# Three post norms of a transformer kernel, each in two halves of the tokens

## The chip, the cores and the metric

The kernel runs on one core of one Trainium2 chip. Its time is device time in microseconds (us). The engines of the core work side by side and meet only at semaphores: PE is TensorE (matmuls, with the weight loads beside them as PEld), DVE is VectorE, ACT is ScalarE, POOL is GpSimd, SP is SyncE, whose queue issues the DMAs. Before the change three runs took 2310.77, 2310.92 and 2311.61 us; the median is 2310.92 us.

## The reference

The input is 512 tokens of 1024 numbers. Two blocks follow each other. The first has a hybrid mixer, a gated MLP, a convolution block and another gated MLP. The second, which holds the change, is

```python
def second_block(x, ...):
    for i in range(DEPTH):                      # DEPTH = 2
        h = rmsnorm(x, norm_mixer_pre[i])
        if i % N_MIXERS == 0:
            m = diff_attention(h, ...)
        else:
            m = short_conv(h, conv_w_in[j], conv_w[j], conv_w_out[j])
        x = x + rmsnorm(m, norm_mixer_post[i])
        h = rmsnorm(x, norm_mlp_pre[i])
        x = x + rmsnorm(sq_relu_mlp(h, mlp_w_up[i], mlp_w_down[i]), norm_mlp_post[i])
    return x
```

with `rmsnorm(x, g) = x * rsqrt(mean(x*x) + EPS) * g` over the 1024 features of a token, `sq_relu_mlp(x) = square(relu(x @ w_up)) @ w_down` with a hidden width of 4096, and `short_conv(x) = (b * conv3(c * v)) @ w_out`, where b, c and v are the three thirds of `x @ w_in`. A post norm needs the sum of squares over all features of a token, so it can't start for a token before the last feature block of the projection ahead of it is done. Tokens don't depend on each other in a norm.

## The kernel before

Everything lies transposed: features on the 128 partitions in 8 blocks k of 128 (`KB = 8`), the 512 tokens along the free dimension. `h` is the residual stream. A projection is a row of weight tiles; one tile is 128 output features by 1024 inputs. The 384 tiles (`NT`) are streamed from HBM into a ring of four slots (`RING = 4`), so tile n+4 takes the slot of tile n. ACT rounds a tile to its high part `whi` (`split_hi`), DVE subtracts to get the low part `wlo` (`split_lo`). `split_hi(Tile(n))` and `split_lo(Tile(n))` prepare tile n+4; the first waits until PE is done with tile n. An activation is split in the same way into `xh` and `xl` (or `yh` and `yl`). PE takes three matmuls of 512 columns for each block of a tile (hi by hi, hi by lo, lo by hi), 24 for a tile. The result of a tile lies in one of eight PSUM banks.

Each engine runs its instructions in the order in which its function issues them; a wait holds up all that is behind it on that engine. There is no scheduler: the order is the order of the code, and every counter of a semaphore is written out.

The last five stages are mlp0 (64 tiles), sc (the short convolution: 24 tiles in, 8 out), and mlp1 (64 tiles), with a post norm at the end of each. At such an end, before the change:

- PE runs the 8 last tiles (`down`, called by `to_m`), DVE adds each to `m` (`add_to_m`, or `set_m` in sc), ACT squares it, POOL sums the squares into `acc`. After the eighth tile PE adds up over the partitions with a matrix of ones (`row_sum_halves`, L1798 to L1803), ACT makes the root (`inv_rms_halves`), DVE scales `m` and adds it to `h` (`post_norm`, L951 and L955), ACT makes `xh` (`post_stage`, L471 to L476), DVE makes `xl` (`pre_lo`, L922).
- PE starts the next stage with `first_round`: four tiles at once, block by block as blocks of `xh` and `xl` appear, in banks 0 to 3. Six matmuls that compute nothing (`keep_clock(6)`, L1822) stand in front. At its end stands `row_sum` (L1787, L1788), the sum for the next stage's own pre norm.
- PE goes on with `second_round`: tiles 4 to 7 of the stage in banks 4 to 7. The pre norm is applied late, when DVE takes a tile out of PSUM and multiplies it by `rrow`. So DVE can't take out the first tile before the sum of `row_sum` has gone through ACT (L421, L423).
- The next tiles' weights hang on this too. DVE prepares tiles 4 and 5 of the stage ahead of that wait (`AHEAD = 2`). Tile 6 is prepared behind it: in mlp1 after the third tile was taken out and squared (`up`, L1570 to L1578), in sc after the first three tiles were taken out and convolved (`short_conv`, L928 to L1641). In both the instruction is L916.

After the last tile of mlp1 the end of the kernel follows: `last_norm` on DVE, `residual` and `result` on PE (sums with the identity matrix, f32), copies by ACT (L905), additions by POOL, and eight output DMAs of 256 KB on SP (L379).

Of the kernel before, what the change touches and what calls it, by code (L numbers as in the profile page):

```python
# [130 lines left out]
def build(nc, x_t, stream, w_glr, w_gate, vecs, consts, taps, out_t):  # L131
    with ExitStack() as ctx:
# [127 lines left out]
        for n in ("exact_ready sb_sph sb_spl wglr_in wglr_hi wglr_lo q_hi q_lo glt_ready glr_done warm warm_done first_hi first_lo gq_done gate_x gate_act la_ready suf_ready "  # L260
                  "kd_ready kend_ready dec_ready upd_ready state_ready go_ready gsq_ready gsum_ready "
                  "gln_ready grr_ready gt_ready gy_ready silu_r "
                  "sb_sq sb_sum sb_ln sb_rr sb_qn sb_vp sb_z sb_abs sb_exp sb_ln2 sb_sp sb_acc sb_w "
                  "sv_half dv_half sb_o sb_yh sb_yl wo_early wo_added "
                  "taps_in u4_in0 u4_in1 u4_in2 pw_t1 pw_t2 pw_sg pw_u pw_zero u4_act u4_pool cv_pe cv_chain cv_done piv_mm piv_ready cen_ready cen_sq "
                  "ln_s1 ln_acc mean_mm mean_neg mean_sq ln_var cen_again ln_t ln_s "
                  "lam_s lam_e lam_ready "
                  "da_sh da_shs da_rc da_qn da_vh da_s da_max da_exp da_rcp da_r1 da_t da_a da_T da_aT da_o da_sq da_sum "
                  "da_ln da_rr da_ot do_part do_sum sc_u sc_y sc_zero").split():
            s(n)  # L270
        for n in ("ff_silu", "ff_hid", "mlp_hid"):
            s(n)
        for n in ("halves_act", "halves_dve", "sum_half"):
            s(n)
# [21 lines left out]
        BY_HALVES = ("da", "mlp0", "sc", "mlp1")  # L296
# [16 lines left out]
        def _(sp):  # L313
# [57 lines left out]
            for k in range(KB):  # L371

                if k in LAST_PE:
                    sp.wait_ge(h_added_act, LAST_PE.index(k) + 1)
                elif k in LAST_DVE:
                    sp.wait_ge(h_added, 8 * 3 + LAST_DVE.index(k) + 1)
                else:
                    sp.wait_ge(h_added_pool, LAST_POOL.index(k) + 1)
                sp.dma_start(out_t[k * P:(k + 1) * P, :], h[:, k]).then_inc(stored, 16)  # L379
            sp.wait_ge(stored, 16 * KB)  # L380
# [3 lines left out]
        def _(act):  # L384
# [339 lines left out]
            act.wait_ge(s("mean_mm"), 1)  # L724
# [101 lines left out]
            def to_m(t0, which):  # L826

                for k in range(KB):
                    t = Tile(t0 + k)
                    if k == KB - 1:  # L830
                        split_hi(t)
                        last_square_halves(which, t.count)
                    else:
                        act.wait_ge(evac_done, t.count)
                        square_block(which + "_post", k, A["m"][:, k])
                        split_hi(t)
                inv_rms_halves(which, LAST_ROOT if which == "mlp1" else None)
# [11 lines left out]
            def mlp(f, t0):  # L849
# [4 lines left out]
                inv_rms(name, D, preload=False, bank=7)  # L854
# [25 lines left out]
            post_stage("mlp0", "sc", T_SC)  # L880
# [5 lines left out]
            inv_rms("sc", D, preload=False, bank=7)  # L886
# [14 lines left out]
            post_stage("sc", "mlp1", T_MLP1)  # L901
            mlp(1, T_MLP1)
            for n, k in enumerate(LAST_PE):
                act.wait_ge(h_summed, n + 1)
                act.activation(h[:, k], ps[:, LAST_BANK[k]], ACT.Copy).then_inc(h_added_act, 1)  # L905
# [3 lines left out]
        def _(dve):  # L909
# [9 lines left out]
            def pre_lo(name, k):  # L919

                dve.wait_ge(xh_ready, 8 * PRE[name] + k + 1)
# [54 lines left out]
            def last_norm():  # L976

                a = 8 * POST["mlp1"]
                dve.wait_ge(s("halves_act"), half_done("mlp1", "root"))
                dve.scalar_tensor_tensor(A["m"][:, 0, A_HALF], A["m"][:, 0, A_HALF], col("post", a), LAST_ROOT[:, A_HALF],  # L980
                                         ALU.mult, ALU.mult).then_inc(s("halves_dve"), 1)
                dve.wait_ge(rrow_ready, SUM["mlp1_post"] + 1)
                dve.scalar_tensor_tensor(A["m"][:, 0, B_HALF], A["m"][:, 0, B_HALF], col("post", a), LAST_ROOT[:, B_HALF],
                                         ALU.mult, ALU.mult).then_inc(post_t, 1)
                for k in range(1, KB):
                    t = ps[:, 6] if k in LAST_DVE else A["m"][:, k]
                    dve.scalar_tensor_tensor(t, A["m"][:, k], col("post", a + k), LAST_ROOT, ALU.mult,
                                             ALU.mult).then_inc(post_t, 1)
                    if k in LAST_DVE:
                        dve.wait_ge(post_t, a + k + 1)  # L990
                        dve.tensor_tensor(h[:, k], t, h[:, k], ALU.add).then_inc(h_added, 1)


            dve.memset(acc[:], 0.0).then_inc(s("warm"), 1)
# [32 lines left out]
            dve.wait_ge(s("glt_ready"), 1)  # L1027
# [44 lines left out]
            dve.wait_ge(s("sv_half"), 1)  # L1072
# [153 lines left out]
            dve.memset(A["ub"][:, :, 0:PAD], 0.0).then_inc(s("pw_zero"), 1)  # L1226
# [14 lines left out]
            def gated(b):  # L1241
# [3 lines left out]
                dve.wait_ge(s("pw_zero"), 1)  # L1245
# [38 lines left out]
            def pivot():  # L1284
                dve.wait_ge(s("piv_mm"), 1)
# [7 lines left out]
            def sum_values(k):  # L1293

                dve.wait_ge(s("cen_ready"), k + 1)
                if k == 1:
                    dve.wait_ge(s("piv_mm"), 1)
# [60 lines left out]
            dve.wait_ge(s("mean_mm"), 1)  # L1358
            dve.tensor_scalar(A["mu"][:], ps[:, 7], -1.0 / D, None, ALU.mult).then_inc(s("mean_neg"), 1)
            dve.wait_ge(s("mean_neg"), 1)  # L1360
# [13 lines left out]
            for k in range(KB):  # L1374
                dve.wait_ge(s("cen_again"), k + 1)
# [25 lines left out]
            for r in range(2):  # L1401
# [3 lines left out]
                for t in range(TB):  # L1405
                    if r == 1 and t == 0:
                        dve.wait_ge(s("dv_half"), 1)
# [121 lines left out]
            def set_m(t, k, halves=False):  # L1529
                dve.wait_ge(tile_done, t.count)  # L1530
                if halves:
                    dve.tensor_copy(A["m"][:, k, A_HALF], ps[:, t.slot, A_HALF]).then_inc(s("halves_dve"), 1)
                    dve.tensor_copy(A["m"][:, k, B_HALF], ps[:, t.slot, B_HALF]).then_inc(evac_done, 1)
                else:
                    dve.tensor_copy(A["m"][:, k], ps[:, t.slot]).then_inc(evac_done, 1)
                split_lo(t)

            def add_halves(t, k):
                dve.wait_ge(tile_done, t.count)
                for c, done in ((A_HALF, s("halves_dve")), (B_HALF, evac_done)):  # L1540
                    dve.tensor_tensor(A["m"][:, k, c], ps[:, t.slot, c], A["m"][:, k, c], ALU.add).then_inc(done, 1)
                split_lo(t)
# [14 lines left out]
            def mlp(f, t0):  # L1557
# [25 lines left out]
                up(0, 0, AHEAD)  # L1583
                up(0, 1, bank=RING)
# [10 lines left out]
                for k in range(KB - 1):  # L1595
                    add_to_m(Tile(t0 + 56 + k), k)
                add_halves(Tile(t0 + 56 + KB - 1), KB - 1)

            mlp(0, T_MLP0)
            post_norm("mlp0", "sc")  # L1600


            dve.memset(A["uc"][:, :, 0:2], 0.0).then_inc(s("sc_zero"), 1)
# [6 lines left out]
            def short_conv(i, ahead=0):  # L1610
                def bank(c):
                    return c % RING + (RING if i == 0 and RING <= c < 2 * RING else 0)

                for u in range(4):
# [8 lines left out]
                    dve.wait_ge(s("sc_zero"), 1)  # L1623
# [23 lines left out]
            for k in range(KB):  # L1647
                set_m(Tile(T_SCO + k), k, k == KB - 1)
            post_norm("sc", "mlp1")
            mlp(1, T_MLP1)  # L1650
            last_norm()
# [3 lines left out]
        def _(pool):  # L1655
# [57 lines left out]
            for name in ("da_post", "mlp0_post", "sc_post", "mlp1_post"):  # L1713
                sum_squares(name)
            for k in LAST_POOL:
                pool.wait_ge(post_t, 8 * POST["mlp1"] + k + 1)
                pool.tensor_tensor(h[:, k], h[:, k], A["m"][:, k], ALU.add).then_inc(h_added_pool, 1)
# [835 lines left out]
```

## Time and profile before

| | |
|---|---|
| median of three runs | 2310.92 us |
| the profiled execution | 2311.71 us |
| its span, first to last instruction | 2309.9 us |
| around the span | 1.8 us |
| PE busy | 2286.0 us, 99% |
| DVE busy | 1283.1 us, 56% |
| ACT busy | 823.5 us, 36% |
| POOL busy | 96.6 us, 4% |
| granted TensorE clock | 1.000 |

The end of a matmul is modelled in the profile, with the time that it takes to drain, so matmuls overlap in it: a 512-column matmul is shown with 0.39 us, while the next starts 0.23 us after it. How long PE takes for something is therefore read from starts. A 99% busy PE hides gaps in which it waits for a new stage. In the rows, L is the line of the kernel, and `x4` counts instructions that were merged. An f32 matmul with the matrix of ones or the identity is recorded as two (`x2`).

### The profile page before, as it was taken

How to read it: one execution, taken by the hardware profiler on the slowest of the kernel's cores; microseconds unless marked ns; L12 is line 12 of the kernel's file. 1: busy time of each engine (PE TensorE's matmuls, PEld its weight loads, DVE VectorE, ACT ScalarE, POOL GpSimd, SP SyncE). 2: the span in 40 equal slices, each digit the busy share in tenths (PEclk: the TensorE clock that was granted, in tenths of full speed). 3: DMA queues.
4: the chain of work that ended last, by engine and by line, in shares of the span. 5: the costliest groups of instructions: out<-in, count | busy, mean ns of one | idle time of the engine just before them, and what ended most of it. 6: DMA issues, size and time to landing. Idle time of an engine off the chain costs nothing.

```text
span 2309.9 us, 29030 instructions
## 1 busy us (share of the span) xinstructions
PE 2286.0 (99%) x10627; PEld 1836.2 (79%) x10627; DVE 1283.1 (56%) x1680; ACT 823.5 (36%) x1137; POOL 96.6 (4%) x82
## 2 busy tenths in 40 slices
PE   9999999999999999999999999999999999999999
PEld 7876888888865888888887777888887887888887
DVE  5453643444598654444547868554456755654453
ACT  5376532322423532322334555222224223322222
POOL 0000000000000000000004311000001001000002
PEclk9999999999999999999999999999999999999999
DMA  5210332332464233232332112323322332333321
GB/s 199 83 46 28 102 106 93 100 100 91 165 176 110 74 100 98 93 100 91 108 102 72 48 46 74 119 95 96 100 91 68 116 99 73 110 94 98 100 91 55
DMA packets 64792, 220.00 MB, mean 95 GB/s; under 512 B 8576, under 2 KB 8960, under 8 KB 64448
## 3 DMA queue, kind: packets, MB, share of 16 engines
q1 hardware_dynamic: 64704, 218.78, 29.7%
q8 instruction: 61, 1.00, 0.2%
q14 instruction: 27, 0.22, 0.0%
HBM read 208.56 MB, written 2.10 MB: 91 GB/s over the span
## 4 chain that ended last, share of the span: by engine, by line
PE 88%; DVE 5%; ACT 4%; issue 2%; DMA 0%; POOL 0%; SPq 0%; DVEq 0%; ACTq 0%; POOLq 0%
PE ps L1727 82%; PE ps L2169 2%; PE ps L2289 1%; DVE h L955 1%; PE ps L2034 1%; DVE nm L1442 1%; ACT ex L764 1%; ACT whi L392 0%; ACT xh L476 0%; DVE xl L922 0%; DVE wlo L916 0%; PE ps L2049 0%; DVE spl L1109 0%; DVE acc L944 0%; DVE m L951 0%
## 5 line engine op out<-in xcount | busy, mean ns | idle before, releaser
L1727 PE MATMUL ps<-xh,whi 128*128 128x512 f32 x1752 | 691.6, 395 | 2.1 <-DVE wlo L1000 2.1
L1727 PE MATMUL ps<-xh,wlo 128*128 128x512 f32 x1752 | 683.2, 390 | 0.0
L1727 PE MATMUL ps<-xl,whi 128*128 128x512 f32 x1752 | 682.8, 390 | 0.0
L916 DVE TENSOR_TENSOR wlo<-raw,whi 128x1024 fp32r<-128x1024 f32 x380 | 473.5, 1247 | 229.8 <-ACT whi L392 220.5
L392 ACT ACTIVATE whi<-raw 128x1024 fp32r<-128x1024 f32 x380 | 398.7, 1050 | 478.0 <-PE ps L1727 477.0
L1727 PE MATMUL ps<-yh,whi 128*128 128x512 f32 x1116 | 437.6, 392 | 1.5 <-DVE m L1478 1.0
L1727 PE MATMUL ps<-yh,wlo 128*128 128x512 f32 x1116 | 435.0, 390 | 0.0
L1727 PE MATMUL ps<-yl,whi 128*128 128x512 f32 x1116 | 434.8, 390 | 0.0
L1727 PEld LDWEIGHTS ps<-xh,whi 128*128 128x128 f32 x1752 | 329.5, 188 | 78.0 <-issue 6.5
L1727 PEld LDWEIGHTS ps<-xl,whi 128*128 128x128 f32 x1752 | 329.3, 188 | 69.8 <-issue 3.1
L1727 PEld LDWEIGHTS ps<-xh,wlo 128*128 128x128 f32 x1752 | 329.1, 188 | 68.7
L1727 PEld LDWEIGHTS ps<-yh,whi 128*128 128x128 f32 x1116 | 209.7, 188 | 47.6 <-DVE wlo L916 1.8
L1727 PEld LDWEIGHTS ps<-yl,whi 128*128 128x128 f32 x1116 | 209.7, 188 | 43.6 <-issue 0.7
L1727 PEld LDWEIGHTS ps<-yh,wlo 128*128 128x128 f32 x1116 | 209.6, 188 | 43.6
L860 ACT ACTIVATE yh<-mr 128x512 f32 (+1 forms) x64 | 40.5, 633 | 219.2 <-DVE mr L1570 219.2
L1525 DVE TENSOR_TENSOR m<-ps,m 128x512 f32 (+1 forms) x46 | 31.8, 692 | 128.2 <-PE ps L1727 128.2
L1165 DVE TENSOR_TENSOR h<-ps,h 128x512 f32<-128x512 f32 x56 | 38.7, 691 | 113.1 <-PE ps L1727 113.1
L673 ACT ACTIVATE yh<-th 128x512 f32 x44 | 27.8, 632 | 199.0 <-DVE th L1203 199.0
L1570 DVE SCALAR_TENSOR_TENSOR mr<-ps,rrow 128x512 f32<-128x512 f32 x64 | 44.2, 690 | 94.6 <-PE ps L1727 92.6
L928 DVE TENSOR_TENSOR tu<-ps,rrow 128x512 f32<-128x512 f32 x44 | 30.4, 691 | 72.6 <-PE ps L1727 72.6
L669 ACT ACTIVATE ts<-tg 128x512 f32<-128x512 f32 x44 | 27.8, 632 | 110.5 <-DVE tg L928 110.5
L928 DVE TENSOR_TENSOR tg<-ps,rrow 128x512 f32<-128x512 f32 x44 | 30.4, 691 | 59.4 <-PE ps L1727 45.8
(283 smaller groups left out, 1850.5 us busy)
## 6 DMA issues: line engine op xcount, KB each, us to landing
raw<-stream SPq DMA_DIRECT2D x380, 512.0 KB, 3.5
u<-ub SPq DMA_DIRECT2D x118, 67.0 KB, 2.4
tapw<-taps SPq DMA_DIRECT2D x1, 3584.0 KB, 13.1
h<-x_t SPq DMA_DIRECT2D x8, 256.0 KB, 6.5
raw<-stream SPq DMA_DIRECT2D x8, 256.0 KB, 6.5
out_t<-h SPq DMA_DIRECT2D x8, 256.0 KB, 2.0
const<-consts SPq DMA_DIRECT2D x1, 1025.0 KB, 9.1
vec<-vecs SPq DMA_DIRECT2D x1, 180.0 KB, 9.0
```

Source lines behind the costliest of these rows:

```text
L392: act.activation(whi[:, a.slot], raw[:, a.slot], ACT.Copy).then_inc(whi_ready, 1)
L669: act.activation(A["ts"][:, u], A["tg"][:, u], ACT.Silu).then_inc(s("ff_silu"), 1)
L673: act.activation(block_of(yh, i * 2 + u), A["th"][:, u], ACT.Copy).then_inc(yh_ready, 1)
L764: act.activation(A["ex"][:, p, c, 0:kv], ps[:, 2 + 2 * p + c, 0:kv], ACT.Exp, bias=A["nm"][:, p, c:c + 1], accum_out=A["sm"][:, p, c:c + 1])\
L860: act.activation(block_of(yh, i * 4 + j), A["mr"][:, j % 2], ACT.Square).then_inc(yh_ready, 1)
L916: dve.tensor_tensor(wlo[:, a.slot], raw[:, a.slot], whi[:, a.slot].bitcast(F32), ALU.subtract)\
L928: dve.tensor_tensor(dst, ps[:, bank], rrow[:], ALU.mult).then_inc(evac_done, 1)
L1165: dve.tensor_tensor(h[:, k], ps[:, bank], h[:, k], ALU.add).then_inc(evac_done, 1)
L1525: dve.tensor_tensor(block_of(A["m"], k), ps[:, t.slot], block_of(A["m"], k), ALU.add)\
L1570: dve.scalar_tensor_tensor(A["mr"][:, j % 2], ps[:, bank + t.slot], 0.0, rrow[:], ALU.max, ALU.mult)\
L1727: mm = pe.matmul(out, lhs, rhs, start=first and n == 0, stop=last and n == 2, skip_group_check=skip)
L2169: mm = pe.matmul(ps[32 * i:32 * i + 32, 5 + b % 2], tapw[:, b, i, m], A["u4"][:, b % 3, i, SHIFTS * m:SHIFTS * m + T], start=m == 0, stop= ...
```

## The change

It does four things in the ends of mlp0, sc and mlp1, and in the starts of sc and mlp1. The post norm of the attention (da) and the start of mlp0 stay as they are.

1. The last tiles before a post norm (3 in mlp0 and sc, 4 in mlp1; the table `SPLIT`) are computed in two passes of 256 columns: first the A half (tokens 0 to 255) of all of them, then the B half (256 to 511) of all. The sum of squares and the root are made for A while PE works on B.
2. The norm, the addition to `h`, `xh` and `xl` are made for the eight blocks of A, then for those of B (`post_split`). DVE scales and adds block k before it makes `xl` of block k-1.
3. `first_round` of sc and mlp1 is replaced by `split_round`: the A half of three tiles block by block; the fourth tile joins at k = 4, in the code, and catches up four blocks; then the B half of all four tiles. It uses banks 4 to 7, `second_round` banks 0 to 3. The sum for the B half of the post norm stands after block k = 2. The six matmuls of `keep_clock` are not issued there.
4. The sum for the next stage's pre norm is no longer at the end of the first round but in `second_round`, after the first of its four tiles.

At the end of mlp1 the A halves of all eight blocks are normed, added by POOL and stored while PE still works; only the B halves go the old way (DVE, PE, ACT, POOL). There are 16 output DMAs of 128 KB instead of 8 of 256 KB. Some semaphores are merged or renamed, with no instruction added or taken away.

```diff
+        SPLIT = {"mlp0": 3, "sc": 3, "mlp1": 4}
...
+            def post_split(which, t0, following, add):
...
+                for k in range(first, KB):
+                    sum_half(t0, k, which, A_HALF, add)
+                sum_half(t0, first, which, B_HALF, add)
+                norm_a(0)
+                add_a(0)
+                norm_a(1)
+                add_a(1)
+                lo_a(0)
+                split_lo(Tile(t0 + first))
+                sum_half(t0, KB - 2, which, B_HALF, add)
+                norm_a(2)
+                add_a(2)
+                lo_a(1)
+                split_lo(Tile(t0 + KB - 2))
+                sum_half(t0, KB - 1, which, B_HALF, add)
+                for k in range(3, KB):
+                    norm_a(k)
+                    add_a(k)
+                    lo_a(k - 1)
+                    if k == 3:
+                        split_lo(Tile(t0 + KB - 1))
+                lo_a(KB - 1)
+                norm_b(0)
+                add_b(0)
+                for k in range(1, KB):
+                    norm_b(k)
+                    add_b(k)
+                    lo_b(k - 1)
+                    if k > LAG + 1:
+                        sq_sum(following, k - LAG - 1)
...
-            def second_round(t, free, name):
+            def second_round(t, free, name, bank=RING):
 
                 for j in range(RING):
+                    if j == 1 and bank == 0:
+                        pe.wait_ge(evac_done, free)
+                        row_sum(name, bank=3)
                     if j == RING - 1:
                         pe.wait_ge(ln_ready, SUM[name] + 1)
-                    tile(t.plus(j), RING + j, xh, xl, free=free)
+                    tile(t.plus(j), bank + j, xh, xl, free=free)
...
+            def split_round(t0, name, which):
+
+                base, last = X0[name], t0.plus(RING - 1)
+                for k in range(KB):
+                    pe.wait_ge(x_ready, base - KB + k + 1)
+                    for j in range(RING - 1):
+                        if k == 0:
+                            pe.wait_ge(wlo_ready, t0.plus(j).count)
+                        half_passes(t0.plus(j), RING + j, xh, xl, A_HALF, k)
+                    if k == 2:
+                        post_sum(which, B_HALF)
+                    if k == 4:
+                        pe.wait_ge(wlo_ready, last.count)
+                        pe.wait_ge(ln_ready, SUM[which + "_post"] + 1)
+                        for done in range(4):
+                            half_passes(last, 2 * RING - 1, xh, xl, A_HALF, done)
+                    if k >= 4:
+                        half_passes(last, 2 * RING - 1, xh, xl, A_HALF, k)
+                for k in range(KB - 2):
+                    pe.wait_ge(x_ready, base + k + 1)
+                    for j in range(RING):
+                        half_passes(t0.plus(j), RING + j, xh, xl, B_HALF, k)
+                pe.wait_ge(x_ready, base + KB)
+                for j in range(RING):
+                    for k in range(KB - 2, KB):
+                        mm = half_passes(t0.plus(j), RING + j, xh, xl, B_HALF, k)
+                    mm.then_inc(tile_done, 1)
...
             def to_m(t0, which, y0):
-                down(Tile(t0), y0)
-                row_sum_halves(which)
+                first = KB - SPLIT[which]
+                for j in range(first):
+                    tile(Tile(t0 + j), j % RING, yh, yl, y_ready, y0)
+                for c in (A_HALF, B_HALF):
+                    for j in range(first, KB):
+                        t = Tile(t0 + j)
...
+                        for k in range(KB):
+                            mm = half_passes(t, t.slot, yh, yl, c, k)
+                        mm.then_inc(s("tile_half") if c is A_HALF else tile_done, 1)
+                        if c is B_HALF and j == first:
+                            post_sum(which, A_HALF)
+                if which == "mlp1":
+                    post_sum(which, B_HALF)
```

Where the instructions stand shows two places. The first is PE at the join of the first and the second round of sc. Before, the sum for the pre norm (`ps<-sums,exact`) stands between the last matmul of the first round and the first of the second:

```order
L1727 MATMUL ps<-xl,whi 128x512
L1727 MATMUL ps<-xh,wlo 128x512
L1787 MATMUL ps<-sums,exact 128x512 [waits sum_lo]
L1788 MATMUL ps<-sums,exact 128x512
L1727 MATMUL ps<-xh,whi 128x512 [waits evac_done,wlo_ready]
```

Now, in the same stage, the last matmuls ahead of that sum are those of the second round's first tile, and what follows is its second tile:

```order
L1936 MATMUL ps<-xl,whi 128x512
L1936 MATMUL ps<-xh,wlo 128x512
L1996 MATMUL ps<-sums,exact 128x512 [waits sum_lo,evac_done]
L1997 MATMUL ps<-sums,exact 128x512
L1936 MATMUL ps<-xh,whi 128x512 [waits evac_done,wlo_ready]
```

The sum has moved down by the 24 matmuls of one tile; the third tile of the round (tile 6 of the stage) now starts one tile after the sum, where it started two tiles after it. The second place is DVE at the end of mlp0. Before, after the last block's addition in two halves (L1541) and one tile of weights (`wlo`):

```order
L1541 TENSOR_TENSOR m<-ps,m 128x256 [waits tile_done]
L1541 TENSOR_TENSOR m<-ps,m 128x256
L916 TENSOR_TENSOR wlo<-raw,whi 128x1024 [waits whi_ready]
L951 SCALAR_TENSOR_TENSOR m<-m,vec,rrow 128x256 [waits halves_act]
L955 TENSOR_TENSOR h<-h,m 128x256 [waits halves_dve]
L951 SCALAR_TENSOR_TENSOR m<-m,vec,rrow 128x256 [waits rrow_ready]
L955 TENSOR_TENSOR h<-h,m 128x256 [waits post_t]
L951 SCALAR_TENSOR_TENSOR m<-m,vec,rrow 128x512
L922 SCALAR_TENSOR_TENSOR xl<-h,vec,xh 128x512 [waits xh_ready]
```

Now, from the B half of the first of the three split tiles on:

```order
L1062 TENSOR_TENSOR m<-ps,m 128x256 [waits tile_done]
L1074 SCALAR_TENSOR_TENSOR m<-m,vec,rrow 128x256 [waits root_half]
L1079 TENSOR_TENSOR h<-h,m 128x256 [waits post_t]
L1074 SCALAR_TENSOR_TENSOR m<-m,vec,rrow 128x256
L1079 TENSOR_TENSOR h<-h,m 128x256 [waits post_t]
L1083 SCALAR_TENSOR_TENSOR xl<-h,vec,xh 128x256 [waits xh_ready]
L994 TENSOR_TENSOR wlo<-raw,whi 128x1024 [waits whi_ready]
L1062 TENSOR_TENSOR m<-ps,m 128x256 [waits tile_done]
L1074 SCALAR_TENSOR_TENSOR m<-m,vec,rrow 128x256
L1079 TENSOR_TENSOR h<-h,m 128x256 [waits post_t]
L1083 SCALAR_TENSOR_TENSOR xl<-h,vec,xh 128x256 [waits xh_ready]
L994 TENSOR_TENSOR wlo<-raw,whi 128x1024 [waits whi_ready]
```

The weights of the next stage's tiles 1, 2 and 3 (`wlo`, L994) now stand between the halves of the norm, because PE holds their slots until the B half of the down tiles is done.

## Rows read from the trace of the kernel before

**Rows 1.** The page: PE's busy line, and the chain that ended last, by engine.

```profile
PE 2286.0 (99%) x10627; PEld 1836.2 (79%) x10627; DVE 1283.1 (56%) x1680; ACT 823.5 (36%) x1137; POOL 96.6 (4%) x82
...
PE 88%; DVE 5%; ACT 4%; issue 2%; DMA 0%; POOL 0%; SPq 0%; DVEq 0%; ACTq 0%; POOLq 0%
```

**Rows 2.** Timeline of PE, end of mlp0 to sc's second round (start us, duration us).

```profile
1755.83 0.39 PE L1727 MATMUL ps<-yh,whi 128*128 128x512 f32 x1
...
1761.04 0.40 PE L1727 MATMUL ps<-yh,wlo 128*128 128x512 f32 x1
1761.28 0.59 PE L1798 MATMUL ps<-acc,const 128*128 128x256 f32 x2
1761.71 0.60 PE L1799 MATMUL ps<-acc,const 128*128 128x256 f32 x2
...
1766.38 0.28 PE L1840 MATMUL ps<-xh,wlo 128*128 128x256 f32 x1
...
1768.06 0.28 PE L1840 MATMUL ps<-xh,wlo 128*128 128x256 f32 x1
...
1789.14 0.40 PE L1788 MATMUL ps<-sums,exact 128*128 128x512 f32 x1
1789.38 0.39 PE L1727 MATMUL ps<-xh,whi 128*128 128x512 f32 x1
```

**Rows 3.** The same of PE, end of sc to mlp1's second round.

```profile
1941.49 0.40 PE L1727 MATMUL ps<-yh,wlo 128*128 128x512 f32 x1
...
1969.58 0.40 PE L1788 MATMUL ps<-sums,exact 128*128 128x512 f32 x1
1969.81 0.39 PE L1727 MATMUL ps<-xh,whi 128*128 128x512 f32 x1
```

**Rows 4.** Timeline of all engines, post norm of mlp0.

```profile
1762.95 0.70 PE L1801 MATMUL ps<-sq,const 128*128 128x256 f32 x2 [0.65 <-ACT sq L437]
...
1763.69 0.39 ACT L446 ACTIVATE lnb<-ps 128x256 f32<-128x256 f32 x1 [0.48 <-PE ps L1801]
...
1764.56 0.48 DVE L951 SCALAR_TENSOR_TENSOR m<-m,vec,rrow 128x256 f32<-128x256 f32 x1 [0.70 <-ACT rrow L448]
...
1765.08 0.42 DVE L955 TENSOR_TENSOR h<-h,m 128x256 f32<-128x256 f32 x1
1765.42 0.48 DVE L951 SCALAR_TENSOR_TENSOR m<-m,vec,rrow 128x256 f32<-128x256 f32 x1
1765.54 0.51 ACT L471 ACTIVATE xh<-h,vec 128x256 fp32r<-128x256 f32 x1 [0.29 <-DVE h L955]
...
1766.94 0.75 DVE L922 SCALAR_TENSOR_TENSOR xl<-h,vec,xh 128x512 fp32r<-128x512 f32 x1
```

**Rows 5.** Timeline of POOL and DVE: a low part beside POOL, and one without it.

```profile
1757.47 1.30 POOL L1667 TENSOR_TENSOR acc<-acc,sq 128x512 f32<-128x512 f32 x1 [4.15 <-ACT sq L401]
1758.37 1.48 DVE L916 TENSOR_TENSOR wlo<-raw,whi 128x1024 fp32r<-128x1024 f32 x1 [1.65 <-ACT whi L392]
...
1762.63 1.23 DVE L916 TENSOR_TENSOR wlo<-raw,whi 128x1024 fp32r<-128x1024 f32 x1 [0.39 <-ACT whi L392]
```

**Rows 6.** Timeline of DVE: low part of tile 6 in sc and in mlp1.

```profile
1797.96 1.23 DVE L916 TENSOR_TENSOR wlo<-raw,whi 128x1024 fp32r<-128x1024 f32 x1 [0.26 <-ACT whi L392]
...
1977.77 1.23 DVE L916 TENSOR_TENSOR wlo<-raw,whi 128x1024 fp32r<-128x1024 f32 x1 [0.19 <-ACT whi L392]
```

**Rows 7.** The end of the kernel: timelines of PE, DVE, ACT, SP, and the DMAs of L379.

```profile
2296.00 0.40 PE L1727 MATMUL ps<-yh,wlo 128*128 128x512 f32 x1
...
2296.44 0.76 DVE L1541 TENSOR_TENSOR m<-ps,m 128x256 f32<-128x256 f32 x2 [4.76 <-PE ps L1727]
...
2305.51 0.60 ACT L905 ACTIVATE h<-ps 128x512 f32<-128x512 f32 x1 [0.26 <-PE ps L2376]
...
2301.57 5.88 SPq L379 DMA_DIRECT2D out_t<-h  x8
...
DMA to landing us min/median/max: 2.0/2.0/2.5
```

More of the change, by code:

```diff
@@ L826, in to_m @@
             def to_m(t0, which):
-                for k in range(KB):
[L829 to L837, printed above, removed]
+                name, first, root = which + "_post", KB - SPLIT[which], LAST_ROOT if which == "mlp1" else rrow
@@ new lines, in root_b @@
+                def root_b():
+                    act.wait_ge(sum_ready, SUM[name] + 1)
+                    act.activation(lnb[:, B_HALF], ps[:, SUM_BANK, B_HALF], ACT.Ln, scale=1.0 / D, bias=EPS)\
+                       .then_inc(ln_ready, 1)
+                    act.wait_ge(ln_ready, SUM[name] + 1)
+                    act.activation(root[:, B_HALF], lnb[:, B_HALF], ACT.Exp, scale=-0.5).then_inc(rrow_ready, 1)
+                for k in range(first):
+                    act.wait_ge(evac_done, t0 + k + 1)
+                    square_block(name, k, A["m"][:, k])
+                    split_hi(Tile(t0 + k))
@@ new lines, in to_m, with x_a @@
+                for k in range(first, KB):
+                    square_a(k)
+                square_b(first)
+                root_a()
+                if which == "mlp1":
+                    for k in range(first + 1, KB):
+                        square_b(k)
+                    root_b()
+                    return
+                following, tn = {"mlp0": ("sc", T_SC), "sc": ("mlp1", T_MLP1)}[which]
+                pre = 8 * PRE[following]
+                def x_a(k):
+                    act.wait_ge(h_added, NORM[which] - KB + k + 1)
+                    act.activation(xh[:, k, A_HALF], h[:, k, A_HALF], ACT.Copy, scale=col("pre", pre + k)).then_inc(xh_ready, 1)
@@ new lines, in x_b @@
+                def x_b(k):
+                    act.wait_ge(h_added, NORM[which] + k + 1)
+                    act.activation(xh[:, k, B_HALF], h[:, k, B_HALF], ACT.Copy, scale=col("pre", pre + k)).then_inc(xh_ready, 1)
+                split_hi(Tile(t0 + first))
+                x_a(0)
+                x_a(1)
+                split_hi(Tile(t0 + KB - 2))
+                square_b(KB - 2)
+                x_a(2)
+                square_b(KB - 1)
+                split_hi(Tile(t0 + KB - 1))
+                x_a(3)
@@ L1975, in _ @@
             wide(Tile(T_SV + 2), 2, 2, 512)
-            wide(Tile(T_SV + 3), 3, 2, 512, order=(2, 3, 0, 1), half=s("sv_half"))
+            wide(Tile(T_SV + 3), 3, 2, 512, order=(2, 3, 0, 1), half=s("v_half"))
             def gla_sum(hd):
```

310 lines of the change are left out of this document (229 added, 81 removed).

## The prediction, before the changed kernel had run

> **What bounds the kernel now.** I read first the page. PE is busy 99% of the span and carries 88% of the chain that ended last [rows 1]; no other engine is near. The kernel is as long as PE's work plus the places where PE waits, and these hide in the busy share. So I went on to the timeline of PE around the two joins that change and the end, and took everything from starts of instructions.
>
> A 512-column matmul takes PE 5.21 us / 23 = 0.2265 us (first to last of one tile, 1755.83 to 1761.04), a tile 24 of them, 5.44 us [rows 2]. The join of mlp0 and sc: the last down matmul is through at 1761.04 + 0.23 = 1761.27, the second round starts at 1789.38, 28.11 us later [rows 2]. In that time stand the 96 matmuls of the first round, 21.74 us. What is left, 6.37 us, is the price of the join: the sum of squares, root, norm, waits, and the sum for the pre norm. In the second join the last down matmul is through at 1941.72 and the round starts at 1969.81: 28.09 us, 6.35 lost [rows 3]. The end: the last down matmul starts at 2296.00, the span ends at 2309.9, 13.9 us [rows 7]. That is all that the change can win: 12.7 us at the joins, part of 13.9 at the end.
>
> **The price of half matmuls.** 256-column matmuls stand in the old first round: fifteen starts, 14 steps, from 1766.38 to 1768.06 make 0.120 us each [rows 2]. Two halves are 0.240, against 0.2265: 0.0135 more for each pair. At each join (3 x 24) + (4 x 24) = 168 pairs cost 2.3 us; at the end 4 x 24 = 96 cost 1.3 us.
>
> **What PE does and waits for at a join.** I laid a timetable from the start of the first A half (t = 0) with the rows' steps. Three A halves 8.64, the first B half to 11.52, the sum for A (two f32 matmuls of 0.43, the step from 1761.28 to 1761.71 [rows 2]) to 12.38, two B halves to 18.14. The second matmul of the sum starts at 11.95; ACT's log 0.74 later, the norm on DVE 0.87 behind it, the addition 0.52 later, `xh` 0.46 later [rows 4]. So the first norm is at 13.56, the addition at 14.08, and the first A block of `xl` can start at 15.3. DVE's steps in a row are 0.40 for a half norm (0.48 shown, less the 0.08 by which a start precedes the end before it, as 1765.08 + 0.42 to 1765.42 shows [rows 4]) and 0.34 for a half addition; `xl` has the form of the norm (0.75 whole, no half in the trace), so I take 0.40. Bounds for it: 0.34, a half addition, and 0.75, the whole. With the wait of 0.12 between norm and addition that is 1.25 us for a block.
>
> Between them stand three weight tiles of about 1.14 (1.23 shown [rows 5]) and two half additions. Tile 2 of the next stage is ready at 19.65, PE wants it at 18.86: 0.8 us of wait. Block 2 is ready at 21.3, block 3 at 23.9, where PE stands at 23.2 after the sum for B: 0.7. With block 4 the fourth tile gives PE 2.9 us of work at once, and from there to the end of the A part it is ahead of nobody: it leaves A at 32.4. DVE begins B at 28.2, and with the sums of squares of the next norm (0.6 each from k = 5) has the last `xl` at 40.9; PE wants it at 41.0. End of the first round: 43.85, of which 1.8 is waiting. The low part of tile 4 comes 0.5 us after that. The second round starts at 44.35. Before, from the same point: 3 x 5.44 + 28.11 = 44.4. **The two are equal.** All that was hidden has been paid for: 6.37 of lost time became 2.3 for half matmuls, 1.7 for the two sums, 2.3 of waits. On top comes the sum for the pre norm, before inside the 28.11 and now behind tile 4: 0.45. Each join: +0.4 us. POOL's half additions are off this path. Their price isn't in the trace: between half of the 1.30 of a whole one and all of it [rows 5]. The last that PE needs has 3 us to spare.
>
> **What the moved sum makes late.** The sum's second matmul in sc starts at 1789.14; the low part of tile 6, which stands behind the first three tiles' work on DVE, starts at 1797.96 and takes 1.23, so it is there at 1799.19, 10.05 us after the sum [rows 2, 6]. Before, PE ran tiles 4 and 5 in that time, 0.24 + 10.88 us, and tile 6 was 1 us early. Now tile 4 stands ahead of the sum, and only tile 5, 0.23 + 5.44 = 5.67, beside the chain. DVE's and ACT's work between is the same, instruction by instruction. PE waits 10.05 + 0.06 - 5.67 = 4.4 us, and 0.1 that I allow for the slower first matmul after a wait: **4.5 us**. In mlp1 the chain is 1977.77 + 1.23 - 1969.58 = 9.42 us [rows 3, 6]: 9.42 + 0.06 - 5.67 + 0.1 = **3.9 us**. Nothing gives it back, since PE is what bounds. In mlp1 DVE is then 5.4 us later with the eight hidden blocks, each 3.3 us of DVE with its weights, and the first down tile needs the last of them; I count 0.4 for it (bounds 0 and 1.5).
>
> sc +4.9, mlp1 +4.7: +9.6.
>
> **The end.** PE has 1.3 more for halves and 0.86 for the sum for A: +2.15. After the last matmul (X): DVE 0.33, ACT 0.79, the second sum matmul 1.25, log 1.99, first norm 2.85 (0.86 after the log). Eight half norms at 0.40, the last at 5.65, the sixth, k = 5, at 4.85; through PE (f32 halves of 0.43) to ACT, done at 6.6. Before, that copy was done at 2306.11, 10.1 after X, and the span ended 3.8 later: three issues on SP's queue and 2.0 to land [rows 7]. With the same 3.8: 10.4, against 13.9. The A halves are stored before; eight more issues of about 0.35 on SP are through by 2 us after X. So -3.5 + 2.15 = -1.35 (bounds -3 and 0, by 0.64 or 1.3 for POOL's last half addition, and whether half DMAs land as whole ones do).
>
> **Sum.** +9.6 - 1.35 = +8.25; I take +8.3. The span becomes 2318.2 and the profiled execution, 1.8 around the span, 2320.0 us. The profiled execution lay 0.8 above the median of the runs; I give 2319.2 for the median.
>
> **Rivals.**
> A. VectorE is slowed by POOL. The low part took 1.48 with POOL still in the first 0.4 us of it, and 1.23 without [rows 5]: 0.25 lost for 0.4 beside. POOL's half additions (0.65 to 1.30) now fall among DVE's half norms, twice at a join: 0.8 to 1.6 us of DVE in the stretch where PE waits on it, and its half steps may each be some 0.05 longer. Together +2 each join: 2323.2. The Trainium skill (GPSIMD Engine Reference, Specifications) says that GpSimd shares its SBUF interfaces with VectorE, and contends with instructions that have two SBUF inputs. All of the half norms, additions and `xl` have two. The row agrees. For: the row. Against: most of the wait in question is short.
> B. Half matmuls cost just half. Then 0.0135 x 432 pairs = 5.8 us go from PE's work. About half of it comes back as waits, as PE stands before the same DVE blocks in the A part: -2.9, 2316.3. Against it stand 14 equal steps of 0.120. The Trainium skill (TensorE: Matmul & The Clock Gate, Back-to-back issue gap) gives a lone warm matmul N/2.4 + 2.5 ns; that is 2.5 ns for each added one, an estimate of 1.1 us for 432, and nearly this case. The row, 13.5 ns, decides against it.
> C. The other side: the kernel gets faster. The mechanism is the third tile of the second round: if its weights were ready when PE comes (the chain behind the sum short of 5.7 us), the 8.4 us of the two waits fall away, and with them the later DVE work: 8.3 - 8.8 = -0.5, no change. To be faster by more than that DVE must also keep ahead in the A part: another 2.3 of waits at each join, -5.1: 2305.8. It decides at 5.7 us; the chains measure 10.05 and 9.42, so this needs an order of instructions that is not the one built.
> D. The waits come as forecast, but the end wins all it can and the A part waits on nobody: 8.3 - 1.5 - 2.5 = +4.3, 2315.2: at the edge of no change.
>
> **Chances.** Forecast 0.70 (its own range 2317 to 2321.5), A 0.15, B 0.05, D 0.07, C 0.03 with both its forms. A change of 0.2% is 4.6 us; less a measurement of this kernel can't tell. Faster: 0.02. Within 0.2%, up to 2315.5: half of D, part of B and C, 0.06. Slower: 0.92. The range from D to A: 2314.8 to 2323.8.
>
> **What would show it.** In the profile after: PE idle of 4 to 5 us before the first matmul of tile 6 of sc, and just under 4 in mlp1, with the low part (DVE, `wlo`) as what ended it; the old 28.1 us of a join, from the last whole down tile to the second round, equal within 1 us; steps of 0.120 between half matmuls also where one tile runs through its eight blocks; 10.4 us after the start of the last down matmul. I would be wrong if tile 6 finds its weights, if half steps are below 0.115 or above 0.125 (each 0.005 is 2 to 4 us over the kernel), or if PE waits for `xl` in the B part, which has only 0.1 us to spare.

## The result, and the profile after

The changed kernel takes 2323.97 us (median of 6 runs, 2321.14 to 2325.57) against 2311.01 for the kernel before (6 runs, 2310.33 to 2311.61): 13.0 us slower, a ratio of 1.0054 with a 95% interval of 1.0041 to 1.0067. I had forecast 2319.2, +8.3, and slower with 0.92; the time lies 0.2 above the upper end of the range, 2323.8. The direction and the places were right, the size was not: what PE pays behind a long wait was put at 0.1 us, and measured 2.97 and 2.57.

The profiled execution took 2324.94 us, its span 2323.2, 13.3 above the span before. The page's busy line and the chain that ended last, as in [rows 1]:

```profile
PE 2291.8 (99%) x11031; PEld 1859.0 (80%) x11031; DVE 1290.9 (56%) x1738; ACT 829.0 (36%) x1158; POOL 102.2 (4%) x97
...
PE 87%; DVE 7%; ACT 4%; issue 2%; DMA 0%; POOL 0%; SPq 0%; DVEq 0%; ACTq 0%; POOLq 0%
```

PE has 404 matmuls more and is still 99% busy. The new thing is in the chain: VectorE went from 5% to 7%. What PE waits for in the last 620 us says where (idle us in all, how often, the longest):

```profile
PE ps L1936 <- DVE wlo L994: 10.6, 6, 4.2
PE ps L1936 <- DVE xl L1083: 0.9, 2, 0.5
PE ps L2104 <- ACT sq L856: 0.5, 1, 0.5
PE ps L2657 <- DVE m L1160: 0.5, 1, 0.5
```

10.6 us are waits for low parts of weights, in six places. The timeline of PE shows them, first the join of mlp0 and sc, then sc's second round (start us, duration; to be read beside [rows 2]):

```profile
1743.90 0.28 PE L1936 MATMUL ps<-yh,whi 128*128 128x256 f32 x1
...
1763.92 0.39 PE L1936 MATMUL ps<-xh,whi 128*128 128x256 f32 x1 [1.02 <-DVE wlo L994]
...
1768.17 0.38 PE L1936 MATMUL ps<-xh,whi 128*128 128x256 f32 x1 [0.46 <-DVE xl L1083]
...
1788.70 0.50 PE L1936 MATMUL ps<-xh,whi 128*128 128x512 f32 x1 [0.32 <-DVE wlo L994]
...
1794.50 0.39 PE L1997 MATMUL ps<-sums,exact 128*128 128x512 f32 x1
...
1799.99 0.39 PE L1936 MATMUL ps<-xh,wlo 128*128 128x512 f32 x1
1804.59 0.80 PE L1936 MATMUL ps<-xh,whi 128*128 128x512 f32 x1 [4.21 <-DVE wlo L994]
1805.18 0.63 PE L1936 MATMUL ps<-xl,whi 128*128 128x512 f32 x1
...
1810.30 0.63 PE L1936 MATMUL ps<-xl,whi 128*128 128x512 f32 x1
1810.73 0.44 PE L1936 MATMUL ps<-xh,wlo 128*128 128x512 f32 x1
```

From the first A half, 1743.90, to the second round, 1788.70, are 44.80 us; before, from the start of the same three tiles, it was 44.43, to 1789.38 [rows 2]. So the join is equal within 0.4. The sum for the pre norm now stands at 1794.50, behind tile 4, and tile 5 runs until 1799.99 + 0.23. Then PE waits 4.37 us for the low part of tile 6, until 1804.59 (the 4.21 in the row counts from the modelled end of the last matmul). Behind this wait stands what I had not counted: fourteen steps from 1804.59 to 1810.73 take 6.14 us where fourteen of 0.2265 take 3.17. The same in mlp1 (beside [rows 3]):

```profile
1988.98 0.39 PE L1936 MATMUL ps<-xh,wlo 128*128 128x512 f32 x1
1992.96 0.79 PE L1936 MATMUL ps<-xh,whi 128*128 128x512 f32 x1 [3.59 <-DVE wlo L994]
1993.55 0.63 PE L1936 MATMUL ps<-xl,whi 128*128 128x512 f32 x1
...
1998.25 0.54 PE L1936 MATMUL ps<-xh,whi 128*128 128x512 f32 x1
```

A wait of 3.75 us, then twelve steps in 5.29 us where 2.72 would do. The windows of PE say why (stretch, PE busy and matmuls, granted clock, DMA share, GB/s):

```profile
1800.00:1804.00 4.00, 0.38 (x2) 1.00 0.00 0
1804.00:1808.00 4.00, 3.41 (x8) 0.50 0.49 152
1808.00:1812.00 4.00, 4.00 (x13) 0.65 0.71 242
...
1988.00:1992.00 4.00, 1.37 (x7) 0.97 0.00 0
1992.00:1996.00 4.00, 3.04 (x7) 0.50 0.38 131
1996.00:2000.00 4.00, 4.00 (x13) 0.68 0.38 131
```

After the wait the granted clock is 0.50, that is 1.2 instead of 2.4 GHz, and it comes back to 2.4 GHz within the next of these stretches. The matmuls ran at half speed, in steps of 0.427 us.

What holds the low part of tile 6 is the chain on VectorE. Its first and last link in sc:

```profile
1796.23 0.69 DVE L1006 TENSOR_TENSOR cc<-ps,rrow 128x512 f32<-128x512 f32 x1 [5.84 <-ACT rrow L436]
...
1803.31 1.23 DVE L994 TENSOR_TENSOR wlo<-raw,whi 128x1024 fp32r<-128x1024 f32 x1 [0.25 <-ACT whi L405]
```

VectorE stood idle 5.84 us for the root of the pre norm, which needs PE's late sum. The same place before the change:

```profile
1790.87 0.69 DVE L928 TENSOR_TENSOR cc<-ps,rrow 128x512 f32<-128x512 f32 x1 [0.98 <-ACT rrow L423]
```

The low part is ready at 1804.54, 10.04 us after the second matmul of the sum started at 1794.50. Before, this chain was 10.05 [rows 2, 6]: nothing in it changed, it only starts later by one tile of PE's work, 5.4 us.

The end of the kernel, of PE, DVE, ACT and SP (beside [rows 7]):

```profile
2313.23 0.28 PE L1936 MATMUL ps<-yh,wlo 128*128 128x256 f32 x1
...
2315.21 0.38 ACT L868 ACTIVATE lnb<-ps 128x256 f32<-128x256 f32 x1 [0.79 <-PE ps L2104]
...
2316.04 2.83 DVE L1160 SCALAR_TENSOR_TENSOR m<-m,vec,ps 128x256 f32<-128x256 f32 x7 [2.08 <-ACT ps L871]
...
2319.00 0.82 ACT L983 ACTIVATE h<-ps 128x256 f32<-128x256 f32 x2 [0.48 <-PE ps L2657]
...
2317.36 4.02 SPq L392 DMA_DIRECT2D out_t<-h  x8
...
DMA to landing us min/median/max: 1.7/1.8/1.9
```

From the last matmul to the end of the span are 9.97 us (before 13.9). These stores, the B halves, land in 1.8 us in the median where whole ones took 2.0.

### The profile page after: what moved, and what is told of

It reads as the page before. It is cut to its first block, busy times and chain, and to the rows that moved or that the text cites. A ratio compares the mean times of both kernels' runs of the same rounds, so it can differ in the third digit from the quotient of the medians.

```text
span 2323.2 us, 29964 instructions
## 1 busy us (share of the span) xinstructions
PE 2291.8 (99%) x11031; PEld 1859.0 (80%) x11031; DVE 1290.9 (56%) x1738; ACT 829.0 (36%) x1158; POOL 102.2 (4%) x97
## 3 DMA queue, kind: packets, MB, share of 16 engines
q8 instruction: 64, 1.05, 0.2%
## 4 chain that ended last, share of the span: by engine, by line
PE 87%; DVE 7%; ACT 4%; issue 2%; DMA 0%; POOL 0%; SPq 0%; DVEq 0%; ACTq 0%; POOLq 0%
PE ps L1936 81%; PE ps L2431 2%; DVE wlo L994 1%; ACT whi L405 1%; PE ps L2551 1%; PE ps L2296 1%; DVE nm L1615 1%; ACT ex L777 1%; PE ps L2311 0%; DVE spl L1282 0%; DVE acc L1022 0%; ACT sph L611 0%; PE ps L2276 0%; DVE m L1089 0%; PE ps L2541 0%
## 5 line engine op out<-in xcount | busy, mean ns | idle before, releaser
L1936 PE MATMUL ps<-xh,whi 128*128 128x512 f32 (+1 forms) x1832 | 711.7, 388 | 12.2 <-DVE wlo L994 10.6
L1936 PE MATMUL ps<-xh,wlo 128*128 128x512 f32 (+1 forms) x1832 | 701.7, 383 | 0.0
L1936 PE MATMUL ps<-xl,whi 128*128 128x512 f32 (+1 forms) x1832 | 701.6, 383 | 0.0
L994 DVE TENSOR_TENSOR wlo<-raw,whi 128x1024 fp32r<-128x1024 f32 x380 | 472.6, 1244 | 223.5 <-ACT whi L405 214.1
L1936 PE MATMUL ps<-yh,whi 128*128 128x512 f32 (+1 forms) x1196 | 451.8, 378 | 1.5 <-DVE m L1651 1.0
L1936 PE MATMUL ps<-yh,wlo 128*128 128x512 f32 (+1 forms) x1196 | 448.5, 375 | 0.0
L1936 PE MATMUL ps<-yl,whi 128*128 128x512 f32 (+1 forms) x1196 | 448.4, 375 | 0.0
L1936 PEld LDWEIGHTS ps<-xh,whi 128*128 128x128 f32 x1832 | 346.1, 189 | 89.1 <-DVE wlo L994 13.1
L1936 PEld LDWEIGHTS ps<-xl,whi 128*128 128x128 f32 x1832 | 346.0, 189 | 68.5 <-issue 3.1
L1936 PEld LDWEIGHTS ps<-xh,wlo 128*128 128x128 f32 x1832 | 345.6, 189 | 67.6
L1936 PEld LDWEIGHTS ps<-yh,whi 128*128 128x128 f32 x1196 | 225.2, 188 | 44.9 <-DVE wlo L994 1.8
## 6 DMA issues: line engine op xcount, KB each, us to landing
tapw<-taps SPq DMA_DIRECT2D x1, 3584.0 KB, 11.3
```

What stands on the lines that cost most here:

```text
L994: dve.tensor_tensor(wlo[:, a.slot], raw[:, a.slot], whi[:, a.slot].bitcast(F32), ALU.subtract)\
L1936: mm = pe.matmul(out, lhs, rhs, start=first and n == 0, stop=last and n == 2, skip_group_check=skip)
```

## The experiments

Each ran beside the kernel before, which took 2310.72 (27 runs) beside the filler, the earlier sum, the earlier weights and the end alone, and 2311.18 (27 runs) beside the other four. All differences are to that. Behind each median stand the ratio to the kernel before and its 95% interval. Where an expectation counts the runs, the second is the earlier sum and the fourth the end alone.

**Is the slow stretch a cost of its own?** PE is given matmuls that nobody reads while it waits for tile 6.

```diff
                         row_sum(name, bank=3)
+                    if j == 2 and bank == 0:
+                        keep_clock(18 if name == "sc" else 15, 2)
                     if j == RING - 1:
```

> The changed kernel with matmuls that compute nothing put where PE waits for the low part of tile 6: 18 of 512 columns in sc, 15 in mlp1 (4.1 and 3.4 us at 0.2265). Theory 1 (the wait is fixed by DVE's chain, and the half clock behind it follows from PE's idleness): the first matmul of tile 6 starts where it did (4.4 and 3.75 us after tile 5), but at full clock; the 14 and 12 slow matmuls (0.427 for 0.2265, 2.8 and 2.4 us) go, so 2324.0 - 5.3 = 2318.5, and less spread between runs. Rival (the slow stretch is not caused by the wait but comes by chance, or by what the A and B halves do to PE): it stays, 2324.

2320.06 us (5 runs, 2319.63 to 2320.92), 1.0041 [1.0027 to 1.0054]. Its timeline in sc's second round:

```profile
1800.23 4.25 PE L2031 MATMUL ps<-exact 128*128 128x512 f32 x18
1804.62 0.50 PE L1936 MATMUL ps<-xh,whi 128*128 128x512 f32 x1
1804.96 0.40 PE L1936 MATMUL ps<-xl,whi 128*128 128x512 f32 x1
```

Tile 6 starts when it did before, 1804.62 against 1804.59, and the second matmul comes 0.34 later instead of 0.59. The span is 2318.1, 5.1 below that of the changed kernel; the two stretches had cost 2.97 + 2.57 = 5.54, and some 0.3 of a new short wait in mlp1's first down tile is in it. By the medians it is 3.9, less than the 5.3 that I had expected: that came from the profiled execution of the changed kernel, which lay 1.0 above its median. All five executions had a mean granted clock of 1.000, where the six of the changed kernel had 0.997 to 0.999, and they lie within 1.3 us instead of 4.4. All this shows that the half clock is a cost beside the wait: tile 6 comes no earlier, only PE's idleness ahead of it was taken away, and the slow stretch is gone with it.

**Is it the sum's place?** The sum for the pre norm goes ahead of tile 4.

```diff
-                    if j == 1 and bank == 0:
+                    if j == 0 and bank == 0:
```

> The changed kernel with the sum for the pre norm back ahead of the second round's first tile (one character: j == 0). Theory 1 (the sum placed behind tile 4 makes tile 6's weights late): both waits of 4.4 and 3.75 go, and the two clock dips with them; PE instead waits some 1.2 us at each join until DVE has the totals (low part of tile 4, then the sums), of which 0.5 was there already. 2324.0 - 8.1 - 5.3 + 1.4 = 2312.0. Rival (theory 2: the joins themselves became slower through half matmuls and DVE's half steps, the late sum costs little): at most a third of the 13 us comes back, 2319 or more.

2312.43 us (11 runs, 2311.99 to 2313.31), 1.0008 [0.9999 to 1.0017]. PE's waits in it, over the same 620 us:

```profile
PE ps L1996 <- DVE sums L1011: 2.2, 2, 1.1
PE ps L1936 <- DVE wlo L994: 2.0, 2, 1.0
PE ps L1936 <- DVE xl L1083: 0.9, 2, 0.5
...
```

The two long waits are gone, in their place PE waits twice 1.1 us for the sums, 2.2, where it had waited 0.8 ahead of the second rounds (0.32 and 0.45). So the sum one tile later saves 1.4 us and costs 8.1 of waits and 5.5 of half clock: 12.3 net, where the two spans differ by 2323.2 - 2311.0 = 12.2. The medians differ by 13.0 - 1.7 = 11.3; the profiled execution of the changed kernel lay 1.0 above its median.

**Is it the sum's place alone?** The same move by itself in the kernel before, with none of the halves.

```diff
-                if name:
+                if name == "mlp0":
                     row_sum(name, bank=7)
...
                 for j in range(RING):
+                    if j == 1 and name != "mlp0":
+                        row_sum(name, bank=7)
```

> The kernel before with one edit: in sc and mlp1 the sum for the pre norm stands behind the second round's first tile, still in bank 7; whole joins, whole end. Theory 1: the two waits for tile 6's low part appear alone, 4.5 and 3.9 us, with a stretch of half clock behind each (2.8 and 2.4), less the 0.5 that PE now waits for the totals, and perhaps 0.4 before the first down tile: 2310.7 + 8.4 + 5.2 - 0.6 = 2323.7. Rival (the late sum hurts only beside the new joins, where DVE is late anyway): 2315 or less.

2322.57 us (5 runs, 2321.74 to 2322.99), 1.0047 [1.0033 to 1.006]: +11.4, where I had expected +13. Nearly the whole loss stands in a kernel that has no other part of the change. Its waits and the stretch behind the one in sc:

```profile
PE ps L1727 <- DVE wlo L916: 7.8, 2, 4.2
```

```profile
1800.39 0.39 PE L1727 MATMUL ps<-xh,wlo 128*128 128x512 f32 x1
1804.98 0.50 PE L1727 MATMUL ps<-xh,whi 128*128 128x512 f32 x1 [4.21 <-DVE wlo L916]
...
1805.86 0.63 PE L1727 MATMUL ps<-xh,whi 128*128 128x512 f32 x1
...
1808.42 0.63 PE L1727 MATMUL ps<-xh,whi 128*128 128x512 f32 x1
...
1809.20 0.40 PE L1727 MATMUL ps<-xh,wlo 128*128 128x512 f32 x1
```

The wait is the same as in the changed kernel (4.2 in the brackets), but here the half-speed steps begin only behind the third matmul and are over by 1809.20: 1.7 us lost in sc and 1.45 in mlp1 instead of 2.97 and 2.57. The same wait is thus followed by slow stretches of different length. In the changed kernel this goes with the time: its three executions with a mean granted clock of 0.997 took 2324.57 to 2325.57, the one with 0.998 took 2323.36, the two with 0.999 took 2321.14 and 2321.26. In this kernel it doesn't: two with 0.997 took 2322.57 and 2322.95, three with 0.999 took 2321.74 to 2322.99. What sets the length was not found.

**Or is it how far the weights are ahead?** Four tiles of weights instead of two are split ahead of the wait for the root of the pre norm, in sc and mlp1; the sum stays where the change put it.

```diff
-                for j in range(1, AHEAD):
+                for j in range(1, 4 if f else AHEAD):
                     split_hi(Tile(t0 + j))
...
-            for j in range(1, AHEAD):
+            for j in range(1, 4):
                 split_hi(Tile(T_SC + j))
```

(and so on VectorE and in the first calls of `up` and `short_conv`, which skip what is then split already).

> The changed kernel with the weights of tiles 6 and 7 of sc and mlp1 prepared ahead of the wait for the root, as those of tiles 4 and 5 are; the sum stays behind tile 4. Theory 1: the waits and the dips go, and no new wait comes in their place; what is left against the kernel before is +0.4 and +0.5 for the joins, 2 x 0.45 for the sum and -1.8 for the end, together 0: 2311.0. Theory 2: as in the run before, 2319 or more.

2312.82 us (11 runs, 2312.13 to 2313.44), 1.0008 [0.9999 to 1.0017]. The long waits go here too, with the sum left late. I had expected 2311.0; 1.3 of the difference is a wait that I had not seen, in mlp1's first down tile, ahead of its last block:

```profile
1998.55 0.50 PE L1938 MATMUL ps<-yh,whi 128*128 128x512 f32 x1 [1.10 <-DVE yl L1742]
```

The wait ends with VectorE's low part of a hidden block; that VectorE is late because it has two more tiles to split first is argued, not shown. Two repairs that have nothing in common but the mechanism, an earlier sum and earlier weights, give the same time within 0.4 us.

**The end alone.** Only mlp1's last norm is in two parts; both joins are as before.

```diff
-        SPLIT = {"mlp0": 3, "sc": 3, "mlp1": 4}
+        SPLIT = {'mlp1': 4}
```

(and the counters, banks and paths that let an unsplit end stand beside a split one).

> Only the last post norm, at the end of mlp1, in two halves; the ends of mlp0 and sc and the starts of sc and mlp1 as in the kernel before. Theory 1 (PE pays 2.15 us for 96 split matmuls and one sum, the way after the last down matmul shrinks from 13.9 to 10.0): 2311.0 - 1.8 = 2309.2. Rival (the end's gain in the changed kernel's trace is an effect of something else, or the 16 output DMAs eat it): 2311 or more.

2309.01 us (11 runs, 2308.6 to 2310.58), 0.9993 [0.9984 to 1.0002]: -1.7. The interval still takes in no change, so the gain rests on the rows as well, the first A half and the last matmul:

```profile
2273.45 0.28 PE L1974 MATMUL ps<-yh,whi 128*128 128x256 f32 x1
...
2297.22 0.28 PE L1974 MATMUL ps<-yh,wlo 128*128 128x256 f32 x1
```

Four split tiles and the sum for A take 2297.22 + 0.12 - 2273.45 = 23.89 us, four whole ones 21.75: +2.14. The span ends at 2307.2, 9.98 behind the last matmul instead of 13.9. That makes 2.14 - 3.92 = -1.8. Against the run with the earlier sum it also gives the two joins: 2312.43 - 2309.01 = +3.4 for both, with 2.2 of waits for the sums in it.

**What a half matmul costs.** In the kernel before, seven of the first eight down tiles of mlp0 and of mlp1 are computed in two passes of 256 columns, 336 pairs, and nothing else is changed.

```diff
-                down(Tile(t0 + 8), y0)
+                tile(Tile(t0 + 8), 0, yh, yl, y_ready, y0)
+                for j in range(1, KB):
+                    t = Tile(t0 + 8 + j)
...
+                    for c in (A_HALF, B_HALF):
+                        for k in range(KB):
+                            mm = passes(ps[:, t.slot, c], w_h[:, k], w_l[:, k], yh[:, k, c], yl[:, k, c],
+                                        c is A_HALF and k == 0, k == KB - 1, skip=True)
```

> The kernel before with one edit: in mlp0 and mlp1, seven down tiles each in the middle of the stage (tiles 9 to 15) are computed in two passes of 256 columns, 336 pairs, with no wait and no other engine's work changed. My price of 0.0135 us for a pair: 2310.7 + 4.5 = 2315.2. Rival (half matmuls cost just half, or 2.5 ns more each): 2310.7 to 2311.6.

2315.76 us (11 runs, 2314.94 to 2316.3), 1.0018 [1.0009 to 1.0027]: +4.6, or 13.6 ns a pair; the forecast had 13.5. One pass of a tile:

```profile
1484.06 0.28 PE L1727 MATMUL ps<-yh,whi 128*128 128x256 f32 x1
...
1486.82 0.28 PE L1727 MATMUL ps<-yh,wlo 128*128 128x256 f32 x1
```

23 steps in 2.76 us, 0.120 each. Why a step takes that long was not tested; each of these matmuls loads its own weights, as the equal counts of PE and PEld in the profile show. The Trainium skill (TensorE: Matmul & The Clock Gate, Back-to-back issue gap) gives N/2.4 + 2.5 ns for an isolated matmul of N columns, and says that this under-counts where N is small. For 336 matmuls more it makes an estimate of 0.8 us; the measurement, 4.6, decides against using it here.

**Who bounds the A part of a join?** On top of the early sum, the third of the first three tiles starts one block later and catches up.

```diff
                     for j in range(RING - 1):
-                        if k == 0:
+                        if j == RING - 2 and k < 1:
+                            continue
+                        if k == 0 and j < RING - 2:
                             pe.wait_ge(wlo_ready, t0.plus(j).count)
+                        if j == RING - 2 and k == 1:
+                            pe.wait_ge(wlo_ready, t0.plus(j).count)
+                            for done in range(1):
+                                half_passes(t0.plus(j), RING + j, xh, xl, A_HALF, done)
```

> The changed kernel with the sum in front (as in the second run) and the third tile joining the first two one block later, so that PE no longer stands 1.0 us before tile 2's low part. Theory 1 (DVE's half steps set the A part, and PE only moves its wait): the 1.0 at each join comes back as a longer wait for xl of block 2 or 3, 2312.4 as without it. Rival (that wait is on PE's path by itself): 2 x 1.0 gained, 2310.4.

2312.6 us (11 runs, 2312.07 to 2313.26), 1.0005 [0.9996 to 1.0014]: +1.4, where the early sum alone had +1.7. The 2.0 us of the rival are not there, as expected:

```profile
PE ps L1936 <- DVE xl L1083: 2.1, 4, 0.6
PE ps L1996 <- DVE sums L1011: 2.1, 2, 1.1
PE ps L1936 <- DVE wlo L994: 0.3, 2, 0.2
```

The waits for low parts fall from 2.0 to 0.3, those for `xl` rise from 0.9 to 2.1. What PE does first is not the limit; VectorE's blocks are.

**The end with three tiles.** From the kernel with the end alone:

```diff
-        SPLIT = {'mlp1': 4}
+        SPLIT = {'mlp1': 3}
```

(and one half addition less on VectorE and on POOL).

> Only the last post norm in halves, as in the fourth run, with three split tiles instead of four. 24 pairs fewer at 0.0135 are 0.3 us; the A halves have 2.9 us less beside PE's work, of which they need none if the 8 half norms (3.3 us) and the stores fit between the root of A and that of B: 2309.0 - 0.3 = 2308.7. Rival (POOL's eight half additions of 0.74 and the stores run past the last down matmul and push the B halves back): 2309.5 or more.

2308.96 us (11 runs, 2308.59 to 2309.52), 0.999 [0.9981 to 0.9999]: -2.2, the lowest median of all that ran, though only 0.05 below that with four tiles; its lead over the kernel before, 0.1%, is smaller than the 0.2% that I set for a sure difference. Its last matmul and the stores of its B halves:

```profile
2296.86 0.28 PE L1972 MATMUL ps<-yh,wlo 128*128 128x256 f32 x1
...
2300.99 4.04 SPq L399 DMA_DIRECT2D out_t<-h  x8
```

With a span of 2306.8 the end is 9.94 us behind that start, as with four tiles (9.98), for 24 pairs of halves fewer.

## Why the prediction was right, and where it fell short

**The waits for tile 6: right.** Forecast 4.4 and 3.8 before the allowance, measured 4.37 and 3.75. The chains of 10.05 and 9.42 that set them were unchanged.

**The step that failed** is "0.1 that I allow for the slower first matmul after a wait". What stands behind such a wait is a stretch at half clock: 2.97 us in sc and 2.57 in mlp1, 5.5 where I had 0.2. I priced the restart by rows of before, where PE's waits are below 1 us, and carried this to waits of 4 without a bound above. The kernel before held a hint: its `keep_clock` puts matmuls that nobody reads into the wait at each join. With a second price for the stretch the sum would have been 13.6. The run with the idle time filled shows that the stretch is a cost of its own.

**The joins: equal as forecast, their price too low.** I had +0.4 each, the sum for the pre norm in it. Measured 0.37 + 0.45 = 0.8 in sc, and in mlp1, where 1932.75 to 1977.69 makes 44.94 against 44.41 before, 0.53 + 0.45 = 1.0. The waits came at their places and in their size: by starts 1.17 for tile 2's low part (0.8), 0.62 for `xl` (0.7), 0.47 before the second round (0.5), 2.26 together in sc where I had 2.3 in all, and 2.41 in mlp1. What is over stands in the steps: behind the first two of these waits and behind two shorter ones the next step of a half matmul takes some 0.22 us instead of 0.12, four times at each join, together 0.4. It is the same 0.1 that I had allowed for tile 6 and left out here.

**Rival A, VectorE slowed by POOL:** it is there and too small. It is one `xl` for each join:

```profile
1761.53 0.92 POOL L1900 TENSOR_TENSOR acc<-acc,sq 128x256 f32<-128x256 f32 x1 [4.23 <-ACT sq L856]
1761.77 0.96 DVE L1083 SCALAR_TENSOR_TENSOR xl<-h,vec,xh 128x256 fp32r<-128x256 f32 x1
```

Elsewhere in the same join they take 0.74 and 0.48. The slow `xl` stands just ahead of tile 2's low part (1762.66), and may be why the wait for that was 1.17 and not 0.8; no run took POOL away, so this is argued only. The waits of the join in all were as forecast. The 2323.2 that A gave is near the result by coincidence.

**Rival B** fell with the run of halves alone (+4.6), **D** with the waits in the joins. **C**, that the kernel is not slower if tile 6's weights are there in time, was rightly held unlikely for this kernel, and its mechanism is confirmed by the two repairs: 2312.4 and 2312.8, +1.7 and +2.1. Its further form, a gain of 5 us, needs VectorE to be ahead at the joins, and the run with the later third tile shows that it is not.

**mlp1's first down tile:** I had 0.4 for VectorE's lateness. It was 0 in the changed kernel, where PE was late itself after its slow stretch, and 0.3 when that stretch was filled, the slower step behind the wait in it.

**The end:** forecast 2.15 - 3.5 = -1.35, measured 2.14 - 3.92 = -1.8 by the rows of the run alone and -1.7 by its median. The half stores land in 1.8 us, 0.2 less than whole ones, which I had as one of the bounds.

In all, by the two profiled executions: joins 1.8, waits 8.1, half clock 5.5, end -1.8, together 13.6 against 13.3 in the span. The two agree less well than it looks: ahead of everything that changed, the trace of the changed kernel is 1.05 us early (its first split tile starts at 1743.90, the same tile before at 1744.95), and behind that it takes 0.7 more than these terms. Neither is placed. The range was 0.2 too narrow: its upper end was a rival's time, the forecast's own range ended at 2321.5, and its own term had no bound above.

## What to carry to other kernels

A small operation moved down an in-order queue by one tile delays all the work that other engines have queued behind its consumer; here 0.45 us of sum, 5.4 us later, held back weights that had been 1.1 and 1.7 us early, and cost 11.4 us. A wait of about 4 us on a busy PE costs itself and a stretch at half clock behind it, 1.5 to 3 us here, so price both. Splitting a norm in two by tokens won, some 2 us of 2311, only where nothing but the end follows; between two stages the half matmuls, extra sums and short waits ate what it hid.

## What the runs showed of the hardware that I had not expected

Waits of 3.75 and 4.37 us of PE, in a stream that was otherwise busy, were each followed by 12 to 14 steps of 0.427 us or more instead of 0.2265 in the changed kernel, at a granted clock of 0.50. In the kernel before with the sum moved, the same waits were followed by fewer such steps, 1.7 and 1.45 us lost instead of 2.97 and 2.57, and in sc they began only behind the third matmul. Waits up to 1.1 us (in the brackets) were followed by none. Eighteen and fifteen matmuls in the waits avoided the stretches.

Behind a wait at full clock the next step is longer too: 0.34 instead of 0.2265 us behind the filler, 0.23 instead of 0.12 between half matmuls behind the wait of 1.02.

An `xl` of 256 columns on VectorE took 0.96 instead of 0.48 us while POOL's addition, itself 0.92 instead of 0.74, ran beside it for 0.68. In [rows 5] a low part lost 0.25 for 0.4 beside POOL.
